# Moving the second memory's keys and values from the first projection stage into the differential attention

## The chip, the core and the metric

The kernel runs on one core of one Trainium2 chip, as one launch. The metric is the device time of the launch in microseconds (us). Three runs of the kernel before gave 3126.4, 3129.0 and 3129.66 us; their median, 3129.0 us, is the time before. Engines are named as the profile names them: PE is TensorE's matmul, PEld its weight load, DVE VectorE, ACT ScalarE, POOL GpSimd, SP SyncE, which issues most transfers here.

## What is computed

The reference is a chain of three blocks over 256 tokens of 1024 features. Only the first block is touched by the change. It has two layers: layer a with a differential attention, layer b with a gated recurrence. Both layers also attend to the same 256 memory rows, each with a norm gain and a projection of its own:

```python
def memory_attention(q_mem, mem, mem_norm_g, w_mem_kv):
    kv = rms_norm(mem, mem_norm_g) @ w_mem_kv          # 256 x 1024 @ 1024 x 512
    k, v = jnp.split(kv, 2, axis=-1)                   # 4 heads of 64
    s = jnp.einsum('bshd,bmhd->bhsm', q, k) * (MEM_HEAD_DIM ** -0.5)
    return einsum('bhsm,bmhd->bshd', softmax(s), v)

def diff_attention_mixer(h, mem, ...):                 # layer a
    q, k, v, qm = split(h @ w_in)                      # 768 + 768 + 768 + 256 columns
    o = rms_norm(diff_attention(q, k, v, lam, ...), subln_g) * (1 - lam_init)   # 6 heads, 2 softmaxes each
    om = memory_attention(qm, mem, a_mem_norm, a_w_mem_kv)
    return concat([o, om]) @ w_out

def hgrn2_mixer(h, mem, ...):                          # layer b, after a dense feed-forward
    ...
    om = memory_attention(qm, mem, b_mem_norm, b_w_mem_kv)
    return concat([o, om]) @ w_out
```

The keys and values of layer b's memory depend on nothing but the inputs, so they may be computed at any time before layer b's memory attention.

## The kernel before

The kernel is a row of stages. A stage is one block of instructions for every engine, written out by hand in the order in which each engine does them; between engines there are semaphores, and a stage begins on an engine only when all engines have ended the stage before it (in the trace this wait reads `PEq L171` or the like). Nothing is reordered by a scheduler.

Weights come through one stream (class `Stream`). Every 1024 x 512 piece of a weight matrix is a panel of 2 MB. SP loads panels in the order in which `s.add(...)` lists them into a ring of three slots (L305); the load of a panel waits until the panel three before it has been used. Since products are made of two rounded parts each, ACT copies half a panel, 128x2048, into `w_hi` (L349, `round_weights`), DVE subtracts that from the panel and writes the rest to `w_lo` (L358, `rest_of_weights`), and PE makes three passes: high by high, high by low, low by high (L470, `products`). Two buffers hold the two halves of a panel, so half 0 of the next panel can be prepared once half 0 of this one has been multiplied. The last thing a stage prepares is half 0 of the next stage's first panel (`first_of_next`); half 1 is prepared when the next stage opens (`open_stage`). A finished panel lies in a pair of PSUM banks and is copied out by ACT or DVE (`evict`).

The stages in question, in their order:

- `setup`: loads, constants, and the rounded parts of the memory under both gains, `mem_a_hi/lo` and `mem_b_hi/lo`. PE ends it with 54 transposes of the identity that compute nothing (`turn_identity`, L597).
- `mem_kv`: two panels, `a_w_mem_kv` and `b_w_mem_kv`, each 96 matmuls of 128x256: first 48 that give keys (kind F), then 48 that give values (kind T). Beside them stand the steps of `input_scales`: the sums of squares of the input x (ACT L828), after the first panel, and the roots (ACT L840), the reciprocal (DVE L846) and the scaled identity `diag` (DVE L849), after the second.
- `in_a`: turns x into features, 32 matmuls with `diag` (PE L689), rounds them (ACT L707, DVE L714), then multiplies five panels of `a_w_in`, 480 matmuls.
- `diff_attention` (function `attention`): 16 units, 12 of the differential attention (two softmaxes for each of six heads) and 4 of layer a's memory. The engines go through iterations s = 0, 1, 2, ... On PE iteration s holds the scores of unit s (L1273), the turned probabilities of unit s-2 (L1291) and the product with the values of unit s-3 (L1303). On DVE it holds mask and maximum of unit s (L1326, L1332; L1337 for memory units), then the reciprocal and scaling of unit s-1 (L1353, L1359). On ACT it holds the exponentials of unit s (L1396), the copy of the turned probabilities of unit s-2 (L1407) and the copy-out of a finished head (L1415). Scores lie in three PSUM banks in turn, 0, 1 and 6. At s = 2 PE makes 18 transposes of the identity.
- `out_a`: the heads are normalised and two panels of `a_w_out` are multiplied; then `dense`, layer b and the other two blocks follow.

Of the kernel before, what the change touches and what calls it, by code (L numbers as in the profile page):

```python
# [29 lines left out]
ALU = mybir.AluOpType  # L30
# [213 lines left out]
class Stream:  # L244
# [10 lines left out]
    def __init__(self, k):  # L255
        self.k = k
        self.jobs = []
        self.starts = []
        self.flat = []
        self.groups = self.halves = self.pairs = self.elsewhere = 0  # L260
        self.split_last = (0, 0)
        self.at = 0

    def add(self, runs):
        self.jobs.append(runs)
        self.starts.append(len(self.flat))
        for r in runs:

            r.first, r.group, r.halves, r.pairs = len(self.flat), self.groups, self.halves, self.pairs
            r.elsewhere = self.elsewhere  # L270
# [6 lines left out]
            self.groups += r.count // r.acc if r.kind not in ("experts", "routed") else 0  # L277
# [142 lines left out]
    def products(self, pe, m, by_chunk=False):  # L420
# [10 lines left out]
        for h in range(max(r.parts, 1)):  # L431
            kind = r.kinds[h]
# [8 lines left out]
            for o in range(width // P if kind == "F" else r.tiles):  # L441
                if r.kind == "R":
# [33 lines left out]
            if h == 0 and r.parts == 2:  # L476
                last.then_inc(k.first_half_used, 1)
        last.then_inc(k.panel_used, 1)

    def stage(self, name, side=None, extra=(), source=(), features=None, norm=False, heads=None,  # L480
# [7 lines left out]

        def evict(eng, m, which):
            r = m.r  # L490
            if r.on == which and m.j % r.acc == r.acc - 1:
                eng.wait_ge(k.panel_used, m.number + 1)
                q = m.p if r.acc == 1 else m.j // r.acc
                r.evict(nc, k.ps[:, 2 * m.bank:2 * m.bank + 2, :], q).then_inc(k.group_read[m.bank], 1)

        with stage(k, name) as st:
# [77 lines left out]
            @st.block.scalar  # L574
            def _(act):
                self.each_with_next(act, runs, lambda m, halves=(0, 1): self.round_weights(act, m, halves),
                                    lambda m: evict(act, m, "act"), steps.get("act", {}))

            @st.block.vector
            def _(dve):  # L580
                self.each_with_next(dve, runs, lambda m, halves=(0, 1): self.rest_of_weights(dve, m, halves),
                                    lambda m: evict(dve, m, "dve"), steps.get("dve", {}), evict_first=norm)
# [285 lines left out]
def input_scales(k, st):  # L868
# [3 lines left out]
    return {"act": {2: [lambda: squares(0, k.x, junk), lambda: squares(1, k.x, junk)], 3: [roots]},  # L872
            "dve": {2: [first_half], 3: [scales]}}
# [348 lines left out]

def unit(scores, values, scale=1.0, mask=None, causal=False, n=S, factor=None, floor=False):
# [15 lines left out]
def attention(k, name, groups, work, last_turns=0, scaled=True):  # L1239
# [14 lines left out]
    score_banks = (0, 1, 6)  # L1254

    with stage(k, name) as st:
        scores_ready, neg_max_ready, exp_done = st.sem("scores_ready"), st.sem("neg_max_ready"), st.sem("exp_done")
        norms_ready, transposed, pt_ready = st.sem("norms_ready"), st.sem("transposed"), st.sem("pt_ready")
        values_done, out_read, dve_order = st.sem("values_done"), st.sem("out_read"), st.sem("dve_order")

        def scores_of(s):
            return k.ps[:, score_banks[s % 3], :]

        @st.block.tensor
        def _(pe):
            for s in range(n_units + 3):
                if s < n_units:
                    u = units[s][0]
                    if s >= 3:
                        pe.wait_ge(exp_done, s - 2)  # L1270
# [24 lines left out]
                if s >= 3:  # L1295
# [4 lines left out]
                    if first and g >= 2:  # L1300
                        pe.wait_ge(out_read, g - 1)
                    for b, rows, first_token, to in u.blocks:
                        last = nc.tensor.matmul(k.ps[r0:r0 + dv, 4 + g % 2, first_token:S], u.values(b),  # L1303
# [4 lines left out]
            turn_identity(k, last_turns, 7)  # L1308

        @st.block.vector  # L1310
        def _(dve):
            o = Order(dve, dve_order)

# [55 lines left out]
            def outputs(m):  # L1369
                u, g, _, is_last = units[m]  # L1370
                if is_last and groups[g][4] is not None:
                    _, r0, dv, dst, gate = groups[g]
                    dve.wait_ge(values_done, m + 1)
                    nc.vector.tensor_tensor(dst, k.ps[r0:r0 + dv, 4 + g % 2, 0:S], gate,
                                            ALU.mult).then_inc(out_read, 1)

            for s in range(n_units + 4):
# [4 lines left out]
                if s >= 4:  # L1382
                    outputs(s - 4)

        @st.block.scalar
        def _(act):
            for s in range(n_units + 4):
# [21 lines left out]
                if s >= 4:  # L1409
                    m = s - 4  # L1410
                    u, g, _, is_last = units[m]
                    if is_last and groups[g][4] is None:
                        _, r0, dv, dst, _ = groups[g]
                        act.wait_ge(values_done, m + 1)
                        nc.scalar.activation(dst, k.ps[r0:r0 + dv, 4 + g % 2, 0:S], ACT.Copy).then_inc(out_read, 1)  # L1415
# [900 lines left out]
def plan_block1(k, w):  # L2316
# [24 lines left out]
    for i, m in enumerate("ab"):  # L2341
# [3 lines left out]
    s.add(runs)  # L2345
# [7 lines left out]
                                                       half_features(v.qm, scale=0.125)), halves="TF")])  # L2353
    s.add([run("T", w["a_w_out"], 0, v.cat_parts[1:], add_to_residual(k.x), on="dve", count=2, pieces=lambda p: 0)])
# [338 lines left out]
def block1(k, w, c, v):  # L2693
# [14 lines left out]
    attention(k, "diff_attention", groups + memory_groups(k, v.qm, v.km[0], v.vm[0], v.cat), v.work)  # L2708
# [1101 lines left out]
def build(nc, w, c, out, parts=(1, 2, 3)):  # L3810
# [45 lines left out]
    k.group_read = [nc.alloc_semaphore(f"group_read{i}") for i in range(SLOTS)]  # L3856
# [58 lines left out]
```

## Time and profile before

| | us |
|---|---|
| median of three runs | 3129.0 |
| lowest and highest run | 3126.4, 3129.66 |
| span of the profiled execution | 3122.5 |
| stage `mem_kv` on PE, its first matmul to its last | 31.41 to 55.90 |
| stage `in_a` on PE, first `diag` matmul to the last product | 58.74 to 120.87 |
| stage `diff_attention` on PE, from its first score matmul | from 122.69 |

The profile is of one execution. Its page gives the span from the first instruction to the last, 3122.5 us; the three timed runs lie 3.9 to 7.2 us above it, since what stands around the program is in a run's time and not in the span. Over the span PE is busy 97%, DVE 64%, ACT 48%. PE's busy time is modelled from pipelined matmuls, so where it matters the starts of instructions are read, not their ends. A row of the timeline gives the start, the length, the engine, the line, the operation, the tiles and, in brackets, how long the engine was idle before it and what released it.

### The profile page before, as it was taken

The numbers are of one execution on the slowest core, as the hardware profiler recorded it, in microseconds if no ns is written. First come the engines' busy times: TensorE is split into PE (matmuls) and PEld (weight loads), VectorE is DVE, ScalarE is ACT, GpSimd is POOL, SyncE is SP. The second block draws the span as 40 slices with busy tenths as digits, with TensorE's granted clock in tenths as the row PEclk, the third lists the DMA queues.
The fourth block names the chain that finished last, engine by engine and source line by source line (L and its number), as shares of the span: only waits on it lengthen the run. The fifth ranks groups of instructions, "written<-read, shape, count | busy, mean of one in ns | idle before, by whom it ended". The sixth has DMA issues, their size and how long they took to land. (4 is left out here: it accounts for less than half of the span.)

```text
span 3122.5 us, 43115 instructions
## 1 busy us (share of the span) xinstructions
PE 3014.5 (97%) x17959; PEld 2637.2 (84%) x17959; DVE 2007.9 (64%) x2237; ACT 1512.8 (48%) x1692; POOL 24.1 (1%) x41
## 2 busy tenths in 40 slices
PE   7999998899999999999999999999999999999998
PEld 6889897788888899778888888998789798997898
DVE  4547647555455467498898987554555756787755
ACT  4543343334344345477777776443434445432453
POOL 0001000000000000000000000000000000000000
PEclk9999999999999999999999999999999999999999
DMA  5338650065555567599999998541445143345142
GB/s 194 132 124 265 223 185 28 9 242 189 188 189 184 173 211 243 201 361 351 354 363 350 370 349 298 174 145 60 141 167 177 42 162 135 135 152 177 55 169 95
DMA packets 197852, 606.10 MB, mean 194 GB/s; under 512 B 19648, under 2 KB 59401, under 8 KB 154394
## 3 DMA queue, kind: packets, MB, share of 16 engines
q1 hardware_dynamic: 192306, 588.23, 53.0%
q0 software_dynamic: 3872, 12.71, 1.3%
q8 instruction: 142, 2.33, 0.3%
q10 hardware_dynamic: 1480, 2.41, 0.3%
q14 instruction: 52, 0.43, 0.0%
HBM read 602.26 MB, written 1.05 MB: 193 GB/s over the span
## 5 line engine op out<-in xcount | busy, mean ns | idle before, releaser
L2121 DVE TENSOR_TENSOR w_lo<-ring,w_hi 128x2048 fp32r<-128x2048 f32 x336 | 769.7, 2292 | 336.2 <-ACT w_hi L2016 331.0
L2016 ACT ACTIVATE w_hi<-ring 128x2048 fp32r<-128x2048 f32 x336 | 643.1, 1915 | 367.4 <-PE ps L1963 153.4
L358 DVE TENSOR_TENSOR w_lo<-ring,w_hi 128x2048 fp32r<-128x2048 f32 (+2 forms) x209 | 469.4, 2247 | 480.1 <-ACT w_hi L349 479.4
L349 ACT ACTIVATE w_hi<-ring 128x2048 fp32r<-128x2048 f32 (+2 forms) x209 | 392.7, 1881 | 645.1 <-PE ps L470 488.4
L470 PE MATMUL ps<-h_hi,w_hi 128*128 128x256 f32 x1616 | 463.7, 287 | 17.6 <-DVE w_lo L358 10.7
L470 PE MATMUL ps<-h_lo,w_hi 128*128 128x256 f32 x1616 | 459.7, 284 | 0.0
L470 PE MATMUL ps<-h_hi,w_lo 128*128 128x256 f32 x1616 | 459.5, 284 | 0.0
L470 PEld LDWEIGHTS ps<-h_hi,w_hi 128*128 128x128 f32 x1616 | 312.5, 193 | 22.2 <-issue 17.0
L470 PEld LDWEIGHTS ps<-h_lo,w_hi 128*128 128x128 f32 x1616 | 312.6, 193 | 0.3
L470 PEld LDWEIGHTS ps<-h_hi,w_lo 128*128 128x128 f32 x1616 | 312.6, 193 | 0.0
L1926 PE MATMUL ps<-w_hi,h_hi 128*128 128x512 f32 x672 | 266.6, 397 | 1.4 <-DVE w_lo L2121 1.4
L1926 PE MATMUL ps<-w_hi,h_lo 128*128 128x512 f32 x672 | 262.4, 390 | 0.0
L1926 PE MATMUL ps<-w_lo,h_hi 128*128 128x512 f32 x672 | 261.6, 389 | 0.0
L1926 PEld LDWEIGHTS ps<-w_hi,h_lo 128*128 128x128 f32 x672 | 126.1, 188 | 27.2
L1926 PEld LDWEIGHTS ps<-w_hi,h_hi 128*128 128x128 f32 x672 | 126.2, 188 | 26.2 <-DVE w_lo L2121 1.7
L1926 PEld LDWEIGHTS ps<-w_lo,h_hi 128*128 128x128 f32 x672 | 126.4, 188 | 24.9
L1926 PE MATMUL ps<-w_hi,picked_one_hi 128*128 128x512 f32 x336 | 135.4, 403 | 3.9 <-DVE w_lo L2121 3.9
L597 PE MATMUL ps<-ident 128*128 128x128 f32 x1076 | 128.7, 279 | 4.0 <-PEq L171 4.0
L1926 PE MATMUL ps<-w_hi,picked_one_lo 128*128 128x512 f32 x336 | 132.3, 394 | 0.0
L1926 PE MATMUL ps<-w_lo,picked_one_hi 128*128 128x512 f32 x336 | 131.5, 391 | 0.0
L597 PEld LDWEIGHTS ps<-ident 128*128 128x128 f32 x1076 | 122.8, 144 | 8.8 <-issue 7.4
L3280 DVE SCALAR_TENSOR_TENSOR arena<-arena,cols 128x256 f32<-128x256 f32 x288 | 119.8, 481 | 1.5
(539 smaller groups left out, 5544.3 us busy)
## 6 DMA issues: line engine op xcount, KB each, us to landing
ring<-in_moe_w_gate_up SPq DMA_DIRECT2D x224, 1024.0 KB, 4.9
ring<-in_moe_w_down SPq DMA_DIRECT2D x112, 1024.0 KB, 4.9
ring<-in_w_in SPq DMA_DIRECT2D x58, 1024.0 KB, 6.9
ring<-in_w_in_even SPq DMA_DIRECT2D x30, 1024.0 KB, 6.9
ring<-in_dense_w_gate_up SPq DMA_DIRECT2D x22, 1024.0 KB, 7.7
ring<-in_w_in_odd SPq DMA_DIRECT2D x16, 1024.0 KB, 6.7
arena<-in_w_ada POOLq DMA_DIRECT2D x24, 512.0 KB, 4.9
ring<-in_b_w_in SPq DMA_DIRECT2D x12, 1024.0 KB, 6.2
```

Of the source, the lines that this page charges most:

```text
L349: k.nc.scalar.activation(self.part(k.w_hi, b, m), src, ACT.Copy).then_inc(k.hi_ready, 1)
L358: k.nc.vector.tensor_tensor(self.part(k.w_lo, b, m), src, self.part(k.w_hi, b, m).bitcast(F32), ALU.subtract).then_inc(k.lo_ready, 1)
L470: last = nc.tensor.matmul(out, lhs, rhs, start=(opens and c == 0 and i == 0), stop=(closes and c == nk - 1 and i == len(passes) - 1 and (r ...
L597: k.nc.tensor.transpose(k.ps[:, bank, 0:P], k.ident[:, :], k.ident[:, :])
L1926: last = nc.tensor.matmul(k.ps[:, u % 3, :], xs[:, 4 * h + kk, at], w[:, kk, :], start=(h == 0 and kk == 0 and i == 0), stop=(h == 1 and k ...
L2016: nc.scalar.activation(high(g, h), raw(g, h), ACT.Copy).then_inc(k.hi_ready, 1)
L2121: nc.vector.tensor_tensor(low(g, h), raw(g, h), high(g, h).bitcast(F32), ALU.subtract).then_inc(k.lo_ready, 1)
L3280: ins = engine.scalar_tensor_tensor(out[:, c, :], src, w, out[:, c, :], ALU.mult, ALU.add)
```

## The change

The two memory projections are no longer one list of panels. The first, of layer a, is the only panel of `mem_kv`. The second, of layer b, becomes a list of its own between `in_a` and `out_a`, marked as an aside: no stage is built for it, it has a PSUM bank pair of its own (banks 6 and 7), and `attention` does its work in the iterations that `slots = [1, 1, 8, 8]` names: both blocks of keys (48 matmuls) on PE in iteration 1, both blocks of values (48 matmuls) in iteration 8.

With it, in `diff_attention`: ACT and DVE open with half 1 of the memory panel; after iteration 1 they prepare half 0 of `out_a`'s first panel; ACT copies the keys and values out at the end of iteration 9; scores use two PSUM banks instead of three, so the scores of unit s wait for the exponentials of unit s-2 instead of s-3; the 18 transposes of the identity at s = 2 are gone; SP issues in this stage the load that follows in the ring. In `mem_kv`, where only one panel is left, all steps of `input_scales` stand ahead of it.

```diff
@@ Stream.add
-    def add(self, runs):
+    def add(self, runs, aside=False):
@@ Stream.place
-        m.bank, m.before = group % SLOTS, i + group // SLOTS
+        m.bank, m.before = (SLOTS, r.asides + j) if r.aside else (group % SLOTS, i + group // SLOTS)
@@ input_scales
-    return {"act": {2: [lambda: squares(0, k.x, junk), lambda: squares(1, k.x, junk)], 3: [roots]},
-            "dve": {2: [first_half], 3: [scales]}}
+    return {"act": {1: [lambda: squares(0, k.x, junk), lambda: squares(1, k.x, junk), roots]},
+            "dve": {1: [first_half, scales]}}
@@ class Aside (new)
+    def products(self, pe, s):
+        for (q, h, o), at in zip(self.blocks, self.slots):
+            if at == s:
+                self.stream.products(pe, self.place(q), only=(h, o))
+    def prepare(self, s, split):
+        for j in range(2, 2 * len(self.panels) + 1):
+            if self.slots[2 * (j - 2) + 1] != s:
+                continue
+            if j < 2 * len(self.panels):
+                split(self.place(j // 2), (j % 2,))
+            else:
+                self.stream.first_of_next(split)
+    def evict(self, eng, s, which):
+        for q in range(len(self.panels)):
+            if self.slots[4 * q + 3] + 1 == s:
+                self.stream.evict(eng, self.place(q), which)
@@ attention
-    score_banks = (0, 1, 6)
+    score_banks = (0, 1) if aside else (0, 1, 6)
+    held = len(score_banks)
...
+        if aside:
+            @st.block.sync
+            def _(sp):
+                k.stream.ahead(sp)
...
-                    if s >= 3:
-                        pe.wait_ge(exp_done, s - 2)
+                    if s >= held:
+                        pe.wait_ge(exp_done, s - held + 1)
...
+                if aside:
+                    aside.products(pe, s)
...
-                    if m == 0:
+                    if m == 0 and not aside:
                         turn_identity(k, 18, 7)
...
+            if aside:
+                k.stream.open_stage(split)
             for s in range(n_units + 4):
...
+                if aside:
+                    aside.prepare(s, split)
+                    aside.evict(act, s, "act")
@@ plan_block1
-    s.add(runs)
+    s.add(runs[0:1])
     s.add([run("F", w["a_w_in"], 0, k.h, to_features(v.qk, scale=0.125)),
...
+    s.add(runs[1:2], aside=True)
@@ block1
-    attention(k, "diff_attention", groups + memory_groups(k, v.qm, v.km[0], v.vm[0], v.cat), v.work)
+    attention(k, "diff_attention", groups + memory_groups(k, v.qm, v.km[0], v.vm[0], v.cat), v.work,
+              aside=Aside(s, [1, 1, 8, 8]))
```

Line numbers move with the change: L349, L358, L828, L840, L1326 and L1396 of before are L351, L360, L836, L848, L1404 and L1488 of after.

ACT in stage `mem_kv`, before (L349 rounds weights, L828 are the sums of squares, L636 and L647 copy a panel out, L840 are the roots, L171 ends the stage):

```order
L574 UNCONDITIONAL_BRANCH
L349 ACTIVATE w_hi<-ring 128x2048 x2
L636 ACTIVATE arena<-ps 128x512
L647 ACTIVATE arena<-ps 128x512
L828 ACTIVATE ps,stat<-x_tokens 128x512 x4
L349 ACTIVATE w_hi<-ring 128x2048
L636 ACTIVATE arena<-ps 128x512
L647 ACTIVATE arena<-ps 128x512
L840 ACTIVATE stat<-stat 128x1 x2
L171 UNCONDITIONAL_BRANCH
```

The same place after:

```order
L582 UNCONDITIONAL_BRANCH
L836 ACTIVATE ps,stat<-x_tokens 128x512 x4
L848 ACTIVATE stat<-stat 128x1 x2
L351 ACTIVATE w_hi<-ring 128x2048
L644 ACTIVATE arena<-ps 128x512
L655 ACTIVATE arena<-ps 128x512
L171 UNCONDITIONAL_BRANCH
```

Two of the three roundings of weights and one copy-out have left the stage, and the roots have moved from its end to its start.

DVE at the start of `diff_attention`, before (L1326 adds the mask, L1332 takes the maximum, L1353 and L1359 scale the probabilities):

```order
L1310 UNCONDITIONAL_BRANCH
L1326 TENSOR_TENSOR ps<-ps,arena 128x384
L1332 TENSOR_REDUCE soft<-ps 128x1 x2
L1326 TENSOR_TENSOR ps<-ps,arena 128x384
L1332 TENSOR_REDUCE soft<-ps 128x1 x2
L1353 RECIPROCAL soft<-soft 128x2
L1359 TENSOR_SCALAR xn<-xn,soft 128x256
L1359 TENSOR_SCALAR xn<-xn,soft 128x128
L1326 TENSOR_TENSOR ps<-ps,arena 128x384
```

The same place after:

```order
L1385 UNCONDITIONAL_BRANCH
L360 TENSOR_TENSOR w_lo<-ring,w_hi 128x2048
L1404 TENSOR_TENSOR ps<-ps,arena 128x384
L1410 TENSOR_REDUCE soft<-ps 128x1 x2
L1404 TENSOR_TENSOR ps<-ps,arena 128x384
L1410 TENSOR_REDUCE soft<-ps 128x1 x2
L1431 RECIPROCAL soft<-soft 128x2
L1437 TENSOR_SCALAR xn<-xn,soft 128x256
L1437 TENSOR_SCALAR xn<-xn,soft 128x128
L360 TENSOR_TENSOR w_lo<-ring,w_hi 128x2048
L1404 TENSOR_TENSOR ps<-ps,arena 128x384
```

Two subtractions of half a panel now stand in DVE's queue, one ahead of unit 0 and one ahead of unit 2; on ACT a rounding of half a panel (L351) stands at the same two places.

## Rows read from the trace of the kernel before

**Rows 1.** Windows: stretch, length, busy and count of each engine, PEclk, DMA share, GB/s.

```profile
44.70:56.20 11.50, 11.47 (x96) 11.27 (x94) 4.67 (x3) 7.35 (x12) 0.00 (x0) 1.00 0.53 184
122.60:162.80 40.20, 37.02 (x199) 27.25 (x200) 27.69 (x94) 26.05 (x92) 0.00 (x0) 1.00 0.16 52
139.65:144.06 4.41, 4.24 (x23) 3.30 (x22) 3.70 (x13) 2.86 (x12) 0.00 (x0) 1.00 0.01 4
```

**Rows 2.** Timeline of PE: start, length, engine, line, operation; stage `mem_kv` into `in_a`.

```profile
31.41 0.49 PE L470 MATMUL ps<-mem_a_hi,w_hi 128*128 128x256 f32 x1 [4.19 <-PEq L171]
...
44.38 0.28 PE L470 MATMUL ps<-w_hi,mem_a_lo 128*128 128x256 f32 x1
...
55.90 0.28 PE L470 MATMUL ps<-w_hi,mem_b_lo 128*128 128x256 f32 x1
58.74 5.44 PE L689 MATMUL ps<-diag,x_tokens 128*128 128x128 f32 x32 [2.57 <-PEq L171]
63.94 0.36 PE L470 MATMUL ps<-h_hi,w_hi 128*128 128x256 f32 x1
```

**Rows 3.** Timeline of ACT in stage `mem_kv`: a rounding, and the end.

```profile
39.00 1.92 ACT L349 ACTIVATE w_hi<-ring 128x2048 fp32r<-128x2048 f32 x1 [10.70 <-PE ps L470]
...
56.70 0.59 ACT L647 ACTIVATE arena<-ps 128x512 f32<-128x512 f32 x1
57.18 0.48 ACT L840 ACTIVATE stat<-stat 128x1 f32<-128x1 f32 x2
```

**Rows 4.** Timeline of PE: the end of `in_a` and the start of `diff_attention`.

```profile
120.87 0.28 PE L470 MATMUL ps<-h_hi,w_lo 128*128 128x256 f32 x1
122.69 1.54 PE L1273 MATMUL ps<-arena 64*128 64x256 f32 x12 [1.54 <-PEq L171]
124.17 2.18 PE L597 MATMUL ps<-ident 128*128 128x128 f32 x18
...
128.67 0.55 PE L1291 MATMUL ps<-ident,xn 128*128 128x128 f32 x3 [0.59 <-DVE xn L1359]
```

**Rows 5.** Windows: granted clock after the gap at 58.74, and its longest low stretch.

```profile
59.00:62.00 3.00, 3.00 (x15) 3.00 (x15) 0.33 (x1) 0.84 (x2) 0.00 (x0) 0.50 1.05 408
...
482.00:493.00 11.00, 11.00 (x56) 11.00 (x57) 3.77 (x4) 6.60 (x5) 0.00 (x0) 0.53 0.00 0
```

**Rows 6.** Timeline of PE: the same turning into features ahead of the dense stage.

```profile
200.97 3.81 PE L689 MATMUL ps<-diag,x_tokens 128*128 128x128 f32 x32 [0.50 <-PEq L171]
204.54 0.36 PE L1559 MATMUL ps<-h_hi,w_hi 128*128 128x256 f32 x1
```

**Rows 7.** Timeline of ACT: the last rounding of `in_a`, and the start of `diff_attention`.

```profile
115.49 1.92 ACT L349 ACTIVATE w_hi<-ring 128x2048 fp32r<-128x2048 f32 x1 [2.99 <-PE ps L470]
...
122.65 1.28 ACT L1396 ACT_TABLE_LOAD   x1 [0.38 <-PEq L171]
124.88 0.47 ACT L1396 ACTIVATE xn<-ps,soft 128x256 f32<-128x256 f32 x1 [0.95 <-DVE soft L1332]
...
126.00 0.47 ACT L1396 ACTIVATE xn<-ps,soft 128x256 f32<-128x256 f32 x1 [0.21 <-DVE soft L1332]
```

**Rows 8.** Timeline of DVE: subtractions of half a panel, and the start of `diff_attention`.

```profile
117.44 2.29 DVE L358 TENSOR_TENSOR w_lo<-ring,w_hi 128x2048 fp32r<-128x2048 f32 x1 [3.52 <-ACT w_hi L349]
123.62 0.57 DVE L1326 TENSOR_TENSOR ps<-ps,arena 128x384 f32<-128x384 f32 x1 [3.88 <-PE ps L1273]
...
126.54 0.56 DVE L1326 TENSOR_TENSOR ps<-ps,arena 128x384 f32<-128x384 f32 x1
```

**Rows 9.** Timeline of PE, iterations 5 and 6 of `diff_attention`: the settled rhythm.

```profile
133.08 0.55 PE L1291 MATMUL ps<-ident,xn 128*128 128x128 f32 x3 [0.18 <-DVE xn L1359]
...
134.40 0.92 PE L1273 MATMUL ps<-arena 64*128 64x256 f32 x4
```

**Rows 10.** Timeline of ACT, iterations 4 and 5: the last part of unit 4's exponentials.

```profile
132.92 0.20 ACT L1396 ACTIVATION_READ_ACCUMULATOR xn<-ps,soft 128x1 f32 x1
...
134.19 0.48 ACT L1396 ACTIVATE xn<-ps,soft 128x256 f32<-128x256 f32 x1 [0.69 <-DVE soft L1332]
```

More of the change, by code:

```diff
@@ L259, in __init__ @@
         self.flat = []
-        self.groups = self.halves = self.pairs = self.elsewhere = 0
+        self.groups = self.halves = self.pairs = self.elsewhere = self.asides = 0
         self.split_last = (0, 0)
         self.at = 0
-    def add(self, runs):
+    def add(self, runs, aside=False):
         self.jobs.append(runs)
@@ L276, in add @@
             self.flat += [(r, p) for p in range(r.count)]
-            self.groups += r.count // r.acc if r.kind not in ("experts", "routed") else 0
+            self.asides += r.count if aside else 0
+            self.groups += r.count // r.acc if r.kind not in ("experts", "routed") and not aside else 0
             self.halves += r.count * r.parts
@@ L431, in products @@
         for h in range(max(r.parts, 1)):
+            if only and h != only[0]:
+                continue
             kind = r.kinds[h]
@@ L441, in products @@
             for o in range(width // P if kind == "F" else r.tiles):
+                if only and o != only[1]:
+                    continue
                 if r.kind == "R":
@@ L475, in products, with evict @@
                     last = nc.tensor.matmul(out, k.ones_row[0:1, 0:P], row, start=False, stop=True)
-            if h == 0 and r.parts == 2:
+            if h == 0 and r.parts == 2 and (not only or only == (0, 1)):
                 last.then_inc(k.first_half_used, 1)
-        last.then_inc(k.panel_used, 1)
+        if not only or only == (1, 1):
+            last.then_inc(k.panel_used, 1)
+    def evict(self, eng, m, which):
+        k, r = self.k, m.r
+        if r.on == which and m.j % r.acc == r.acc - 1:
+            eng.wait_ge(k.panel_used, m.number + 1)
+            q = m.p if r.acc == 1 else m.j // r.acc
+            r.evict(k.nc, k.ps[:, 2 * m.bank:2 * m.bank + 2, :], q).then_inc(k.group_read[m.bank], 1)
     def stage(self, name, side=None, extra=(), source=(), features=None, norm=False, heads=None,
@@ L1219, with __init__, place, all_read @@
 WHOLE = (0, S)
+class Aside:
+    def __init__(self, stream, slots, late=0, late_parts=None):
+        self.stream, self.slots, self.late, self.late_parts = stream, slots, late, late_parts
+        self.panels = [(r, p) for r in stream.jobs[stream.at] for p in range(r.count)]
+        self.blocks = [(q, h, o) for q in range(len(self.panels)) for h in range(2) for o in range(2)]
+        assert len(slots) == len(self.blocks) and all(r.parts == 2 for r, _ in self.panels)
+    def place(self, q):
+        r, p = self.panels[q]
+        return self.stream.place(r, 0, p)
+    def all_read(self, eng):
+        m = self.place(len(self.panels) - 1)
+        eng.wait_ge(self.stream.k.group_read[m.bank], m.before + 1)
+    def first_read(self, eng):
+        m = self.place(0)
+        eng.wait_ge(self.stream.k.group_read[m.bank], m.before + 1)
+    def products(self, pe, s):
[5 more added lines that the diff above has]
+            if self.slots[2 * (j - 2) + 1] != s:
+                continue
+            if j < 2 * len(self.panels):
[6 more added lines that the diff above has]
+                self.stream.evict(eng, self.place(q), which)
 def unit(scores, values, scale=1.0, mask=None, causal=False, n=S, factor=None, floor=False):
@@ L1236, in unit, with attention @@
     return u
-def attention(k, name, groups, work, last_turns=0, scaled=True):
+def attention(k, name, groups, work, last_turns=0, scaled=True, aside=None):
     nc = k.nc
@@ L1253, in attention, with out_of, gated @@
     diagonals = work[:, 4:6, :].rearrange("p b (t n) -> p b t n", t=TT)
-    score_banks = (0, 1, 6)
+    score_banks = (0, 1) if aside else (0, 1, 6)
+    held = len(score_banks)
+    late = aside.late if aside else 0
+    def out_of(g):
+        _, r0, dv, _, _ = groups[g]
+        return k.ps[r0:r0 + dv, 4 + g % 2, 0:S]
+    def gated(g):
+        return groups[g][4] is not None and g >= late
     with stage(k, name) as st:
@@ L1300, in _ @@
                     if first and g >= 2:
-                        pe.wait_ge(out_read, g - 1)
+                        if g - 2 < late:
+                            pe.wait_ge(out_copied, g - 1)
+                        else:
+                            pe.wait_ge(out_read, g - 1 - late)
                     for b, rows, first_token, to in u.blocks:
-                        last = nc.tensor.matmul(k.ps[r0:r0 + dv, 4 + g % 2, first_token:S], u.values(b),
+                        last = nc.tensor.matmul(out_of(g)[:, first_token:S], u.values(b),
                                                 exps_t[0:rows, m % 2, to:to + S - first_token],
@@ L1411, in _ @@
                     u, g, _, is_last = units[m]
-                    if is_last and groups[g][4] is None:
-                        _, r0, dv, dst, _ = groups[g]
+                    if is_last and not gated(g):
+                        dst = groups[g][3]
                         act.wait_ge(values_done, m + 1)
-                        nc.scalar.activation(dst, k.ps[r0:r0 + dv, 4 + g % 2, 0:S], ACT.Copy).then_inc(out_read, 1)
+                        nc.scalar.activation(dst, out_of(g), ACT.Copy).then_inc(out_copied if late else out_read, 1)
+                if aside:
+                    aside.prepare(s, split)
+                    aside.evict(act, s, "act")
+    if aside:
+        k.stream.at += 1
 def swiglu_run(w_gate_up, w_down, experts, ff):
```

40 lines of the change are left out of this document (23 added, 17 removed).

## The prediction, made before the changed kernel ran

> **What bounds the kernel now.** I read the busy times by stretch first, then PE's timeline through the three stages that the change touches, then ACT's and DVE's beside it. In `mem_kv` PE has matmuls without a break: in the 11.5 us of the second panel it is busy 11.47 us and ACT and DVE are not half busy [rows 1]. So a panel there costs what PE takes for it, and everything else hides under it. In `diff_attention` PE is busy 37.02 of 40.20 us, and in two settled iterations 4.24 of 4.41 us [rows 1]; its only wait there is 0.18 us for DVE's scaling [rows 9]. The waiting is at the start: 18 empty transposes of 2.18 us, and 0.59 us of idleness for DVE's scaling [rows 4]. So the attention is a chain from PE to DVE to ACT to PE at its start, and bound by PE after three iterations. The change takes 96 matmuls from a place where PE bounds and puts 48 where PE waits and 48 where PE bounds. Over the whole span there is nothing to be had beyond this: the rest of the order is unchanged.
>
> **What leaves `mem_kv`.** The second panel's matmuls begin with the one after 44.38 and the last begins at 55.90 [rows 2]: 96 matmuls, 11.52 us, all on the path. Its roundings lay under the first panel and cost nothing there.
>
> **The turn from `mem_kv` to `in_a`.** From the last matmul to the first of L689 it is 55.90 to 58.74, 2.84 us [rows 2]. In it ACT copies the panel out and then makes the roots, from 57.18 [rows 3], and DVE makes `diag`; only then do the engines meet. The roots and `diag` now stand ahead of the one panel, where ACT had no work until 39.00, for 10.70 us [rows 3], 7.6 of them after the stage's first matmul at 31.41 [rows 2], and DVE waits for ACT; so what is left is the copy-out. The turn from `in_a` to `diff_attention` has just that, a last panel copied out in two halves: 120.87 to 122.69, 1.82 us [rows 4]. Gain 1.02 us.
>
> **The clock behind this turn.** After the 2.57 us of idleness before 58.74 PE is granted 0.50, the 1.2 GHz level [rows 5], and L689 lasts 5.20 us until the first product at 63.94 [rows 2]. The same 32 matmuls ahead of the dense stage, after a gap of 0.50 us, take 3.57 us, 200.97 to 204.54 [rows 6]. The gap will be about 1.54 us, as at 122.69, and there the next stretch stayed at 1.00 [rows 1, 4]. I take the gain, 1.63 us; its other end is 0. Together the first product of `in_a` comes 11.52 + 1.02 + 1.63 = 14.17 us earlier. SP's loads move up with it; the first panel of `in_a` takes the ring slot of the memory panel, and its load is issued earlier than before.
>
> **The start of `diff_attention`.** All times here are on the clock of before. ACT's first instruction there begins at 122.65 [rows 7]. That is now half 1 of the memory panel; the subtraction on DVE starts 1.95 us after such a rounding (115.49 to 117.44) and holds DVE 2.29 us, some 2.2 us to the next start [rows 7, 8]. So the first mask starts at 122.65 + 1.95 + 2.2 = 126.8 instead of 123.62 [rows 8]: 3.2 us late. The first exponentials start 1.26 us after the first mask and the second 1.12 us after those [rows 7, 8], so 129.2, and last some 0.9 us: 130.1. Now ACT rounds half 0 of `out_a`'s first panel. It needs the buffer of the key half, so it waits for PE's first 48 matmuls; these start at about 123.7, behind two of the three score groups, and take 11.52 / 2 = 5.76 us: 129.5. They are in time, by 0.6 us, and cost nothing; without that cover each microsecond more would be one more here. ACT starts at 130.1, DVE subtracts at 132.05, and the mask of unit 2 follows at 134.25 instead of 126.54 [rows 8]: **7.7 us late**. Behind DVE's wait stand the scaling of unit 1 and with it PE's second group of transposes, which came 2.13 us after that mask, at 128.67 [rows 4]; now it comes at 136.4. PE has run out of work at about 131.6 (scores 2 and 3 and the first transposes, 2.1 us, after 129.5), so it is idle some 4.8 us.
>
> **The clock behind this stall.** Gaps of 4.19 us at 31.41 and 2.57 us at 58.74 [rows 2] were followed by the low level; this one is longer. At 58.74 the low stretch lost 1.63 us of work. In the attention the units that run in it are bound by PE, so I take 1.6 us, with 0 and 3.4 us (twice the stretch) as ends.
>
> **The second lump.** In iteration 8 PE makes 48 matmuls, 5.76 us, before the transposes of unit 6; ACT and DVE wait for the scores of unit 9. PE had 0.17 us of slack in 4.41 us [rows 1], so nearly all of it is on the path: **5.7 us**. The copy-out in iteration 9 is two ACT instructions of 0.5 us; ACT had 0.69 us of idleness in an iteration [rows 10], so 0.3 us, ends 0 and 1.0.
>
> **Scores in two banks.** Scores of unit 6 start at 134.40 [rows 9]; the exponentials of unit 4, which they will wait for, end at 132.92 + 0.20 = 133.12 [rows 10]. With 1.28 us to spare this costs nothing. SP's load in this stage waits for the second lump; its panel is used only in the dense stage, from 204.54 [rows 6], and lands long before.
>
> **The sum.** Earlier by 14.2, later by 7.7 + 1.6 + 5.7 + 0.3 = 15.3: 1.1 us more. It is made on an execution with a span of 3122.5 us, and the runs lie some 6.5 us above that span at their median; I add it to the median, 3129.0 + 1.1 = **3130.1 us**. What is late at the end of the attention stays late, since `out_a` begins when all engines have ended. A low stretch of the clock more or fewer in a later stage, whose phase moves, would be worth 1.6 us either way.
>
> A rule weighed. In these 40.20 us PEld is busy 27.25 us against PE's 37.02 [rows 1]. The Trainium skill, "Perfetto Trace Analysis", section "Identifying the Most-Contended Engine", says that the busy share of matmuls is no good measure of how close TensorE is to its limit, and that the share of weight loads is to be used. By it the attention would have room for the second lump, and the sum would be the first rival below; the 0.18 us of PE's waiting speaks against it, and the sum goes by that.
>
> **Rivals.**
> 1. *The second lump hides.* PE's weight loads leave 40.20 - 27.25 = 12.95 us in the attention [rows 1], more than a lump. Were that usable, the lump would cost nothing: 15.3 - 5.7 = 9.6 against 14.2, so 3129.0 - 4.6 = 3124.4 us, still within the bound. Against it: engines take their instructions in order, and PE's next start follows the last nearly at once [rows 9].
> 2. *The clock stays low.* PE restarts at 136.4 on a thin diet and keeps the 1.2 GHz level through iterations 4 to 8, as it did for 11 us at 482 to 493 [rows 5]. An iteration's PE work is 2.1 us (half of 4.24) and would be 4.2 against the 2.2 of now: 2.0 us for each of some four more iterations, 8 us: 3138.1 us, **slower**. It decides from the point where the low stretch is some 10 us longer than the one I count. For it: such a stretch exists. Against it: the settled attention ran at 1.00 with PE 96% busy [rows 1].
> 3. *The stall is not paid.* If later iterations took the 7.7 + 1.6 us back, the time would be 3120.8 us, **faster**. For it: ACT has 0.69 us idle in an iteration. Against it: PE would have to run ahead, and its slack over the twelve units is six times 0.17, 1 us.
>
> **How the numbers follow.** Forecast 0.81, rival 1 0.07, rival 2 0.08, rival 3 0.04. A measurement of this kernel tells changes from 0.2%, 6.3 us, on: 3122.7 to 3135.3. Forecast and rival 1 lie within; of the forecast's own spread I give nothing to either side. So faster 0.04, same 0.88, slower 0.08. Bounds: with the stall's clock loss at 0, copy-out 0, the lump at 4.9 (5.7 less 0.17 of slack in each of five pairs of iterations) and a low stretch fewer later, 14.2 - 12.6 + 1.6 = 3.2 us less, 3125.8. With the gain of the first clock term at 0, the second at 3.4, copy-out 1.0 and a low stretch more, 12.5 against 17.8 + 1.6: 6.9 more, 3135.9. Range 3125.8 to 3135.9.
>
> **What would show it.** In the changed profile: the last matmul of `mem_kv` at about 44.4 and L697 about 1.8 us later at full clock (the line of L689 will move by eight); a third mask of the attention about 7.7 us later, counted from the stage's start; a hole in PE of 4 to 5 us ahead of the second group of transposes, then a granted clock of 0.5; iteration 8 longer by 5.7 us. I am wrong if PE has no hole there, if iteration 8 is not longer, or if anything past `out_a` takes another time than before.

## The result, and the profile after

The changed kernel takes 3134.84 us at its median (3131.32 to 3139.34), the kernel before 3127.14 us (3122.53 to 3129.66) over six runs, the three of the forecast among them. The ratio is 1.0033, 95% interval 1.002 to 1.0046: slower, by 7.7 us. The forecast was 3130.1 us with a range of 3125.8 to 3135.9, and called the difference too small to measure. The time lies in the range; the call was wrong. Counted from the time of before, the range went from 3.2 us less to 6.9 us more, and 7.7 us lies outside it: the time falls inside because the kernel before came out 1.9 us lower over six runs than the 3129.0 us of the forecast, which is luck.

The table sets three points of PE's timeline side by side: the first product of `in_a`, the first score of `diff_attention`, and the first empty transpose of `out_a`, which begins when the attention has ended. Times are microseconds from the start of the profiled execution.

| | before | after | difference |
|---|---|---|---|
| first product of `in_a` | 63.94 | 48.32 | -15.6 |
| first score of `diff_attention` | 122.69 | 107.02 | -15.7 |
| end of `diff_attention` | 162.77 | 169.47 | +6.7 |
| length of `diff_attention` | 40.08 | 62.45 | +22.4 |
| span | 3122.5 | 3129.5 | +7.0 |

So nearly the whole difference is made before 170 us: 15.6 us won up to `in_a`, 22.4 us lost in the attention. The end of the attention in the kernel before, which [rows 4] don't show:

```profile
162.77 0.84 PE L597 MATMUL ps<-ident 128*128 128x128 f32 x6 [0.78 <-PEq L171]
```

PE's timeline of the kernel after, at these places (start, length, engine, line, operation; in brackets the idle time before it and what ended it; the answers to [rows 2] and [rows 4]):

```profile
44.76 3.81 PE L697 MATMUL ps<-diag,x_tokens 128*128 128x128 f32 x32 [1.50 <-PEq L171]
48.32 0.36 PE L476 MATMUL ps<-h_hi,w_hi 128*128 128x256 f32 x1
...
107.02 0.93 PE L1343 MATMUL ps<-arena 64*128 64x256 f32 x8 [1.48 <-PEq L171]
107.88 0.39 PE L476 MATMUL ps<-mem_b_hi,w_hi 128*128 128x256 f32 x1
...
114.67 0.55 PE L1363 MATMUL ps<-ident,xn 128*128 128x128 f32 x3
...
120.60 0.90 PE L1363 MATMUL ps<-ident,xn 128*128 128x128 f32 x3 [4.54 <-DVE xn L1437]
...
124.29 0.90 PE L1363 MATMUL ps<-ident,xn 128*128 128x128 f32 x3
...
139.04 0.58 PE L476 MATMUL ps<-w_hi,mem_b_hi 128*128 128x256 f32 x1
...
146.41 0.49 PE L1363 MATMUL ps<-ident,xn 128*128 128x128 f32 x3
...
169.47 0.85 PE L605 MATMUL ps<-ident 128*128 128x128 f32 x6 [0.78 <-PEq L171]
```

The turn from `mem_kv` to `in_a` has a gap of 1.50 us where it had 2.57, and its 32 matmuls last 3.56 us to the first product, at full clock. The first lump, the 48 matmuls of the keys, begins at 107.88, and the first transposes follow it at 114.67. Then PE waits 4.54 us for DVE's scaling. From there on one iteration takes 124.29 - 120.60 = 3.69 us, not the 2.2 us of before (4.41 us for two in [rows 1]), and the three transposes of an iteration 0.90 us, not 0.55. The second lump, the 48 matmuls of the values, takes 146.41 - 139.04 = 7.37 us.

Where the 4.54 us come from stands in DVE's timeline of the kernel after (the answer to [rows 8]; L360 is the subtraction of half a panel, L1404 the mask):

```profile
108.94 2.29 DVE L360 TENSOR_TENSOR w_lo<-ring,w_hi 128x2048 fp32r<-128x2048 f32 x1 [4.82 <-ACT w_hi L351]
111.15 0.56 DVE L1404 TENSOR_TENSOR ps<-ps,arena 128x384 f32<-128x384 f32 x1
...
116.27 2.29 DVE L360 TENSOR_TENSOR w_lo<-ring,w_hi 128x2048 fp32r<-128x2048 f32 x1 [2.12 <-ACT w_hi L351]
118.48 0.56 DVE L1404 TENSOR_TENSOR ps<-ps,arena 128x384 f32<-128x384 f32 x1
```

The third mask starts at 118.48, 11.46 us after the first score at 107.02. Before it was 126.54 - 122.69 = 3.85 us [rows 4, 8]. DVE waits 2.12 us for ACT's rounding and then subtracts for 2.29 us, and the scaling for which PE waits stands behind both.

The clock in the same stretch, by windows of the kernel after (stretch, length, busy time and count of PE, PEld, DVE, ACT and POOL, granted clock, DMA share, GB/s):

```profile
115.00:118.00 3.00, 1.06 (x7) 0.67 (x4) 1.73 (x1) 1.24 (x1) 0.00 (x0) 1.00 0.00 0
118.00:120.60 2.60, 0.00 (x0) 0.00 (x0) 2.50 (x9) 0.87 (x5) 0.00 (x0) 0.62 0.00 0
120.60:139.00 18.40, 18.40 (x55) 14.33 (x55) 9.23 (x32) 7.45 (x29) 0.00 (x0) 0.50 0.00 1
139.00:143.00 4.00, 4.00 (x21) 3.97 (x21) 1.97 (x7) 0.91 (x4) 0.00 (x0) 0.56 0.00 0
143.00:146.40 3.40, 3.40 (x30) 3.40 (x30) 0.00 (x0) 0.00 (x0) 0.00 (x0) 1.00 0.00 0
107.00:169.40 62.40, 56.14 (x276) 44.54 (x276) 32.51 (x96) 30.67 (x95) 0.00 (x0) 0.81 0.20 68
```

The clock falls inside the hole and stays at 0.50, the 1.2 GHz level, for all of the 18.4 us up to the second lump, though PE is shown busy for every one of them. It is back at 1.00 only between 3 and 4 us into that lump. DVE and ACT are each busy about half of that time or less: the stage waits for a slow PE.

The loss of 22.4 us then has three parts. The start is late by 11.46 - 3.85 = 7.6 us. Five iterations at 3.69 instead of 2.2 us cost 7.45 us. The second lump costs 7.37 us, of which 5.84 are its matmuls at full clock (measured below, with `out_a` prepared later) and 1.53 the low clock. The sum is 22.4.

### The profile page after: what moved, and what is told of

Read it like the earlier page. It is cut to its first block and busy times, and to the rows that moved or that the text cites. A ratio compares the mean times of both kernels' runs of the same rounds, so it can differ in the third digit from the quotient of the medians.

```text
span 3129.5 us, 43078 instructions
## 1 busy us (share of the span) xinstructions
PE 3020.2 (97%) x17941; PEld 2640.4 (84%) x17941; DVE 2008.0 (64%) x2237; ACT 1513.0 (48%) x1692; POOL 24.1 (1%) x41
## 5 line engine op out<-in xcount | busy, mean ns | idle before, releaser
L360 DVE TENSOR_TENSOR w_lo<-ring,w_hi 128x2048 fp32r<-128x2048 f32 (+2 forms) x209 | 469.4, 2247 | 475.0 <-ACT w_hi L351 474.3
L351 ACT ACTIVATE w_hi<-ring 128x2048 fp32r<-128x2048 f32 (+2 forms) x209 | 392.7, 1881 | 633.7 <-PE ps L476 474.9
L476 PEld LDWEIGHTS ps<-h_hi,w_hi 128*128 128x128 f32 x1616 | 312.6, 193 | 20.9 <-issue 15.6
```

The lines of the kernel that those rows point to most:

```text
L351: k.nc.scalar.activation(self.part(k.w_hi, b, m), src, ACT.Copy).then_inc(k.hi_ready, 1)
L360: k.nc.vector.tensor_tensor(self.part(k.w_lo, b, m), src, self.part(k.w_hi, b, m).bitcast(F32), ALU.subtract).then_inc(k.lo_ready, 1)
L476: last = nc.tensor.matmul(out, lhs, rhs, start=(opens and c == 0 and i == 0), stop=(closes and c == nk - 1 and i == len(passes) - 1 and (r ...
```

## Experiments

The theory to be tested (A): the hole ahead of the second transposes takes the clock, and the attention's own matmuls, which keep a high clock, don't bring it back; without the hole, or with the clock brought back, only the late start and the second lump are lost. The rivals: the iterations are slow for another reason that the change brought (two score banks instead of three, preparations in the queues of ACT and DVE), or the attention would have fallen low by itself. All runs in one table; the first three number columns are from the profiled execution, in us.

| kernel | end of attention | its length | span | ratio to before, 95% |
|---|---|---|---|---|
| before | 162.77 | 40.08 | 3122.5 | |
| after | 169.47 | 62.45 | 3129.5 | 1.0033 (1.002 to 1.0046) |
| after, run again | 171.59 | 63.13 | 3130.0 | 1.0029 (1.0017 to 1.004) |
| after, hole filled | 163.09 | 53.48 | 3123.3 | 0.9997 (0.9989 to 1.0006) |
| after, `out_a` prepared later | 158.14 | 49.77 | 3119.4 | 0.9993 (0.9985 to 1.0002) |
| after, second lump earlier | 164.33 | 56.08 | 3125.1 | 1.0013 (1.0004 to 1.0022) |
| after, transposes behind the hole | 169.26 | 61.05 | 3127.6 | 1.0011 (1.0001 to 1.0021) |
| before, roots first | 160.71 | 40.58 | 3122.4 | 0.9992 (0.9983 to 1.0001) |
| before, with a hole | 187.98 | 65.23 | 3150.2 | 1.0081 (1.0066 to 1.0096) |

**The hole filled.** In the changed kernel PE gets 38 empty transposes of the identity, into a bank that nothing else uses then, ahead of its wait for the second scaling:

```diff
                     if m == 0 and not aside:
                         turn_identity(k, 18, 7)
+                    if m == 1 and aside:
+                        turn_identity(k, 38, 7)
```

> The changed kernel with 38 transposes of the identity on PE ahead of its second group of transposes, that is in the hole of 4.54 us in which PE waits for DVE; nothing else moves. 38 x 0.12 us = 4.6 us, so they end about when the hole ends. Theory A (the hole drops PE's clock, and the attention's thin work then leaves it at 1.2 GHz until the second lump): the granted clock stays at 1.00 through iterations 2 to 8, an iteration there takes 2.2 us instead of 3.69, and the kernel is some 6 us faster than the changed one: about 3128.5 against 3134.8. Theory B (the lumps and the two score banks keep PE's clock low, hole or not): clock 0.5 again, time within 1 us of the changed kernel's. Theory C (transposes of the identity fill PE's time and yet don't hold its clock): clock 0.5 from about the same place, as in B, and real products in the hole are the next thing to try.

PE's timeline, and the windows of the same stretch (columns as above):

```profile
118.59 4.37 PE L605 MATMUL ps<-ident 128*128 128x128 f32 x38
123.19 0.55 PE L1365 MATMUL ps<-ident,xn 128*128 128x128 f32 x3 [0.24 <-DVE xn L1439]
...
118.60:123.20 4.60, 4.36 (x40) 4.13 (x39) 4.23 (x9) 1.11 (x6) 0.00 (x0) 1.00 0.01 4
123.20:140.00 16.80, 16.44 (x103) 14.04 (x104) 11.02 (x39) 8.36 (x33) 0.00 (x0) 1.00 0.00 0
```

The transposes do nothing but keep PE at work. The second scaling comes no earlier for them, and yet the clock stays at 1.00 and the attention lasts 53.48 us, 9.0 less than in the profile of the changed kernel. What is left over the 40.08 us of before is 13.4: the 7.6 of the start and 5.8 for the lump. The ratio to before is 0.9997, so all of the measured loss is gone, with both lumps, both score banks and all preparations in place. That excludes the first rival. The gain of the change is gone too: it stands level with the kernel before.

**The preparation of `out_a` moved.** ACT rounds and DVE subtracts the first half of `out_a`'s first panel after iteration 7, under the second lump, instead of after iteration 1:

```diff
-            if self.slots[2 * (j - 2) + 1] != s:
+            if self.slots[2 * (j - 2) + 1] + 6 != s:
                 continue
```

> The changed kernel with one number altered: ACT and DVE prepare half 0 of out_a's first panel after iteration 7 instead of after iteration 1, so that it lies under the second lump. Theory A (the stall of DVE behind PE's first lump makes the hole, and the hole makes the long low stretch): no hole over 1 us, clock 1.00, the mask of unit 2 comes about 3.9 us later than before (behind the first lump) instead of 7.7, the attention costs 3.9 + 5.7 + 0.3 = 9.9 us more than before instead of 22, against 14 to 15.6 us gained ahead of it: 4 to 5.5 us faster than the kernel before, about 3122.5. Theory B (lumps keep the clock low): the stall goes but the clock is still 0.5, some 4 us faster than the changed kernel, about 3130.5.

PE's timeline, and windows from the attention's start to the second lump, and over the lump:

```profile
118.26 0.55 PE L1363 MATMUL ps<-ident,xn 128*128 128x128 f32 x3 [0.85 <-DVE xn L1437]
...
129.24 0.39 PE L476 MATMUL ps<-w_hi,mem_b_hi 128*128 128x256 f32 x1
...
135.08 0.49 PE L1363 MATMUL ps<-ident,xn 128*128 128x128 f32 x3
...
108.40:129.20 20.80, 19.59 (x122) 16.39 (x122) 16.17 (x49) 12.73 (x41) 0.00 (x0) 1.00 0.26 99
129.20:135.10 5.90, 5.90 (x50) 5.86 (x50) 3.46 (x5) 2.41 (x4) 0.00 (x0) 1.00 0.00 0
```

The hole shrinks to 0.85 us and the clock does not fall in the attention. The attention lasts 49.77 us, 9.7 more than before: 5.84 for the lump (129.24 to 135.08), and 3.9 by which the third mask is late (116.13 - 108.37 = 7.76 us after the first score, against 3.85 before). That mask no longer waits for a preparation but for PE's scores of its unit, which stand behind the first lump, as was expected:

```profile
116.13 0.57 DVE L1404 TENSOR_TENSOR ps<-ps,arena 128x384 f32<-128x384 f32 x1 [0.62 <-PE ps L1343]
```

The five iterations ahead of the lump take 129.24 - 118.26 = 10.98 us, 2.2 each, as before. In the profile the attention ends 4.6 us earlier than before and the span is 3.1 us shorter; the median is 3121.29 against 3124.58 us, but the interval of the ratio ends at 1.0002, so a gain on the kernel before is not told from none. On the changed kernel it is one: 0.9993 against 1.0033, with intervals that lie apart.

**The second lump moved up.** The two value blocks are projected in iteration 4 instead of 8:

```diff
-              aside=Aside(s, [1, 1, 8, 8]))
+              aside=Aside(s, [1, 1, 4, 4]))
```

> The changed kernel with the second lump, the 48 matmuls of the values, in iteration 4 instead of 8. The hole stays. Theory A, with the low stretch lasting until dense products come: the clock is back at 1.00 some 4 us into that lump, four iterations earlier, each of which then takes 2.2 instead of 3.69 us: 6 us faster than the changed kernel, about 3129, low stretch some 9 to 10 us long instead of 24. Rival (the stretch has its own length, whatever PE does in it): low for 24 us again, so time as the changed kernel's or up to 2 us longer, since the lump then runs at the low clock throughout.

```profile
121.83 0.90 PE L1363 MATMUL ps<-ident,xn 128*128 128x128 f32 x3 [4.54 <-DVE xn L1437]
...
121.80:125.50 3.70, 3.67 (x11) 2.88 (x11) 1.69 (x6) 1.75 (x7) 0.00 (x0) 0.50 0.02 4
125.50:128.00 2.50, 2.50 (x12) 2.48 (x12) 1.97 (x7) 0.92 (x4) 0.00 (x0) 0.51 0.00 0
128.00:132.40 4.40, 4.40 (x39) 4.40 (x38) 0.00 (x0) 0.00 (x0) 0.00 (x0) 1.00 0.00 0
132.40:150.00 17.60, 16.91 (x90) 13.13 (x88) 12.97 (x45) 10.98 (x41) 0.00 (x0) 1.00 0.37 120
```

The hole is the same 4.54 us, and the clock is lost the same way. It is back at 1.00 2.5 us into the lump, which now begins at 125.5 instead of 139.0, and stays there for the iterations behind it. The attention is 6.4 us shorter than in the changed kernel (56.08 against 62.45). So what ends the low stretch is the lump, wherever it stands, and not the number of iterations.

**The roots first, alone.** The kernel before with the one part of the change that moves the squares, roots and `diag` of `mem_kv` to its start; both panels stay there:

```diff
-    return {"act": {2: [lambda: squares(0, k.x, junk), lambda: squares(1, k.x, junk)], 3: [roots]},
-            "dve": {2: [first_half], 3: [scales]}}
+    return {"act": {1: [lambda: squares(0, k.x, junk), lambda: squares(1, k.x, junk), roots]},
+            "dve": {1: [first_half, scales]}}
```

> The kernel before with one part of the change: the sums of squares, roots and scales of the input stand ahead of the first panel of mem_kv; both memory panels stay there, and the attention is untouched. By the prediction's terms the turn into in_a takes 1.82 instead of 2.84 us, and the clock behind it stays at 1.00, which gives 1.0 + 1.6 us: 2.6 us faster than the kernel before, about 3124.5. Rival: ACT, which now rounds half 1 of the second panel after the sums, is late with nothing and nothing is gained but the 1.0 us, since the clock falls after any such turn: 3126.

```profile
57.81 3.81 PE L689 MATMUL ps<-diag,x_tokens 128*128 128x128 f32 x32 [1.50 <-PEq L171]
61.38 0.36 PE L470 MATMUL ps<-h_hi,w_hi 128*128 128x256 f32 x1
...
57.80:61.40 3.60, 3.59 (x33) 3.60 (x33) 1.53 (x4) 2.31 (x6) 0.00 (x0) 1.00 0.98 358
...
120.13 1.54 PE L1273 MATMUL ps<-arena 64*128 64x256 f32 x12 [1.54 <-PEq L171]
121.61 3.85 PE L597 MATMUL ps<-ident 128*128 128x128 f32 x18
125.29 0.49 PE L1291 MATMUL ps<-ident,xn 128*128 128x128 f32 x3
...
121.70:125.10 3.40, 3.40 (x17) 3.40 (x18) 3.29 (x11) 1.82 (x8) 0.00 (x0) 0.50 1.07 358
```

Against [rows 2] the gap is 1.50 instead of 2.57 us, and the first product of `in_a` comes at 61.38 instead of 63.94, 2.56 us earlier: the two terms of 1.02 and 1.63 us together. At the end of the attention 2.06 of them are left, and in the span 0.1. The last rows show why 0.5 us are lost in the attention: here the clock falls at its start, behind a gap of 1.54 us, and is back when the 18 empty transposes end, which take 3.85 us instead of the 2.18 of [rows 4]. So the attention can fall low without the hole, but with these transposes behind the fall it was low for 3.4 us only; they are among what the change takes out. The ratio, 0.9992 (0.9983 to 1.0001), agrees with 2.6 us but does not tell it from none.

**The changed kernel again**, in the runs of the next two:

> The changed kernel itself, once more, beside the two that follow and beside the kernel before. If the long low stretch of PE's clock is what the hole brings on every time, the new profile shows it again, from the hole to the second lump (some 24 us at 0.5), and the time is 6 to 8 us above the kernel before. Rival: the stretch was a chance of that one execution, and this one shows a short stretch of 3 to 7 us, with a time some 3 to 4 us lower.

It measured 1.0029 (1.0017 to 1.004) and repeats the picture: a gap of 4.54 us, the low level behind it, and the high one again only within the second lump. The first product of `in_a`, and windows behind the hole and at the lump's end:

```profile
49.77 0.36 PE L476 MATMUL ps<-h_hi,w_hi 128*128 128x256 f32 x1
...
122.00:145.00 23.00, 22.95 (x76) 18.83 (x77) 11.22 (x39) 8.41 (x33) 0.00 (x0) 0.50 0.00 1
146.00:149.00 3.00, 3.00 (x27) 3.00 (x26) 0.00 (x0) 0.00 (x0) 0.00 (x0) 1.00 0.00 0
```

**A hole in the kernel before.** Two subtractions whose result nothing reads go on DVE behind iteration 1; there is no lump, there are three score banks, and nothing is prepared:

```diff
                 if s >= 4:
                     outputs(s - 4)
+                if s == 1 and name == "diff_attention":
+                    for _ in range(2):
+                        o(nc.vector.tensor_tensor(k.w_lo[:, 1, :], k.w_hi[:, 1, :].bitcast(F32), ...
```

> The kernel before, with nothing of the change, and two idle subtractions of half a panel on DVE after iteration 1 of the differential attention (4.5 us, into a buffer that nothing reads before it is filled anew): a hole in PE of some 5 us at the place of the changed kernel's, with three score banks, 18 empty transposes and no lump anywhere. Theory (a hole drops the clock, and the attention's own work does not bring it back): low from about 128 to the end of the attention or to the next dense stretch, 12 iterations of 3.7 instead of 2.2 us: 4.5 + 15 to 18, some 20 us slower than the kernel before, about 3145. Rival (a low stretch of some 3.4 us, as I had predicted): 4.5 + 1.6, about 3131.

PE's timeline, and the windows of the hole, of the rest of the attention, and of its end:

```profile
133.38 0.90 PE L1291 MATMUL ps<-ident,xn 128*128 128x128 f32 x3 [5.24 <-DVE xn L1359]
...
127.20:133.40 6.20, 0.96 (x6) 0.69 (x5) 6.03 (x10) 0.90 (x5) 0.00 (x0) 0.87 0.25 79
133.40:183.00 49.60, 49.60 (x144) 36.52 (x145) 23.14 (x78) 19.52 (x73) 0.00 (x0) 0.50 0.00 1
183.00:188.00 5.00, 4.05 (x20) 2.00 (x18) 0.00 (x0) 2.64 (x7) 0.00 (x0) 1.00 0.00 0
```

A wait that made PE's transposes 4.7 us later (133.38 against 128.67 in [rows 4]) costs the attention 25.2 us, and the kernel 1.0081 (1.0066 to 1.0096). PE is shown busy for 49.60 of 49.60 us and is granted 0.50 in all of them. Here no lump comes, and the low level lasts until 183.0, 5 us before the stage's end; why it ends there isn't shown. The estimate, some 20 us, was 5 too small: it counted 12 iterations of 3.7 us, and the trace has 13 groups of transposes from the hole to 183.0, and four of the iterations are longer than 4 us. This excludes the second rival, since the same attention without the hole runs at 1.00 [rows 1], or with the roots first is low for 3.4 us at its start, and it shows that no other part of the change is needed for the loss.

**Transposes behind the hole.** The same 38 transposes as in the first experiment, one iteration later, when the clock has already fallen (the condition is `m == 2`):

> The changed kernel with 38 transposes of the identity on PE not in the hole but after it, ahead of the third group of transposes; the hole stays. If PE without a break brings the clock back, whatever it works on: some 4 us into the transposes the clock is at 1.00 again, the transposes cost 5.5 to 6 us, and iterations 4 to 8 take 2.2 us, which saves 6 to 7: within 1 us of the changed kernel. If only dense products do that, the clock stays at 0.5 until the second lump, the transposes take 8 to 9 us, and the kernel is some 8 us slower than the changed one, about 3142.

```profile
121.79 0.90 PE L1365 MATMUL ps<-ident,xn 128*128 128x128 f32 x3 [4.54 <-DVE xn L1439]
125.48 6.71 PE L605 MATMUL ps<-ident 128*128 128x128 f32 x38
132.02 0.49 PE L1365 MATMUL ps<-ident,xn 128*128 128x128 f32 x3
...
121.80:130.00 8.20, 8.20 (x32) 7.39 (x33) 3.62 (x13) 2.62 (x11) 0.00 (x0) 0.50 0.01 2
131.00:140.00 9.00, 8.88 (x53) 7.32 (x52) 5.25 (x18) 3.64 (x13) 0.00 (x0) 1.00 0.00 0
```

Transposes without a break between them bring the clock back as the lump does, and the attention's iterations keep it from then on. The transposes themselves take 6.71 us of PE, so the attention gains only 2.1 us on the changed kernel run beside it (61.05 against 63.13); within 1 us was expected. The median, 3129.42 against 3134.28 us, differs by more than the two profiles do (3127.6 against 3130.0), and the two ratios' intervals overlap a little; only the clock is shown here, not the size of the gain.

## Why the prediction was wrong, by its own steps

**What leaves `mem_kv`, the turn, and the clock behind it: right.** 11.52 + 1.02 + 1.63 = 14.17 us were forecast for the first product of `in_a`. The changed kernel run again has it at 49.77, 14.17 us earlier; the profile above has it at 48.32, 15.6 earlier, because there the first panel of `mem_kv` escaped a low stretch that it had before. The gap forecast at 1.54 us is 1.50, and the clock behind it holds. The start of `mem_kv` after, and the windows of it after and before (columns as above):

```profile
31.52 0.36 PE L476 MATMUL ps<-mem_a_hi,w_hi 128*128 128x256 f32 x1 [3.28 <-PEq L171]
...
31.00:35.00 4.00, 3.48 (x29) 3.51 (x30) 0.51 (x4) 3.16 (x10) 0.00 (x0) 1.00 0.94 352
...
31.00:35.00 4.00, 3.59 (x17) 3.62 (x18) 0.02 (x1) 0.00 (x0) 0.00 (x0) 0.57 0.89 317
```

**The start of `diff_attention`: right.** Forecast late by 7.7 us with an idle PE for some 4.8; measured 7.6 and 4.54.

**The clock behind this stall: this step failed.** It was sized at 1.6 us, at most 3.4, by the low stretch at 58.74, which is followed by 32 feature matmuls and the dense products of `in_a`, one after another. Measured are 7.45 us in five iterations and 1.53 in the lump, 9.0 us, which is also what the attention gains when the hole is filled. The row taken as the measure was of the wrong kind: what the low level costs depends on the work that follows it, and here that is work that does not bring the clock back. That possibility stood beside the forecast as rival 2, with 8 us for iterations 4 to 8, and got a chance of 0.08, on the ground that the settled attention ran at 1.00 with PE 96% busy [rows 1]. This row shows that the attention keeps a clock that it has. It says nothing of whether it regains one that it has lost, and the kernel with a hole alone shows that it doesn't, for 49.6 us. With 9.0 in the place of 1.6 the forecast's sum would have been 1.1 + 7.4 = 8.5 us. The spans differ by 7.0; most of the rest are the 1.4 us that the first panel won beyond the forecast. The low stretch at 482 to 493 [rows 5], which spoke for the rival, was the better row: there PE is shown busy for 11.00 of 11.00 us and is still low.

**The second lump: right.** Forecast 5.7 us on the path; 5.84 at full clock with `out_a` prepared later, which refutes rival 1. The Trainium skill, "Perfetto Trace Analysis", section "Identifying the Most-Contended Engine", would judge TensorE's headroom by the share of its peak that the matmuls reach, which the prediction leaves out, and by its weight loads. By the weight loads the lump had room; the runs don't agree, since 48 matmuls cost their full time in a stage whose weight loads left a third of it free.

**Copy-out and score banks: right.** After the second lump nothing beyond it is lost (9.7 us in the experiment with the later preparation, all of it named above), and with two banks five iterations take 2.2 us each.

**Rival 3, the stall not paid: refuted** by the hole filled, where the 7.6 us of the start are still in the attention's length though all runs at full clock.

**A low stretch more or fewer later: more than was allowed.** From the end of the attention to the end of the program the nine profiles differ from the one of before by up to 2.5 us (with the hole in the kernel before, 25.2 us at the end of the attention and 27.7 at the end); 1.6 us were allowed. Which of them come in an execution was not settled. The medians of the kernel before moved from 3124.58 to 3127.14 us between the runs, so of gains below some 3 us none was shown.

**What stays open.** Why PE's work in the attention holds the higher level but is so slow to regain it. The runs show that within 48 matmuls, or 38 or 18 transposes, in a row the clock comes back, and that 49.6 us of the attention's scores, transposes and values went by before it did. The trace shows no break in PE's work in either, and which of their differences decides was not tried.

## What to carry to other kernels

Work that is moved into a stage where engines take turns has to be priced by what its preparation does in the queues of the other engines: half a panel's rounding and subtraction held up the scaling, and PE with it, for some 4 us. Price such a hole in PE by the work behind it and not by its own length: look for a row in which such work brought the clock back, as 48 matmuls in a row did here, and if there is none, count the whole stretch up to the next work that does. The remedies are cheap: put the preparation where PE has work of its own (under the lump), or fill the hole with empty transposes, and read the granted clock by stretch before believing that a busy PE is a fast one. Either remedy took back the loss here; neither made the change a gain on the kernel before that could be told from none.

## What the runs showed of the hardware

The record of PE as busy for 49.60 of 49.60 us, at a granted clock of 0.50, was not expected; in the same stage and the same kernel, without the hole, it is busy 37.02 of 40.20 us at 1.00 [rows 1]. The hole of 4.54 us, in four profiles, and that of 5.24 us (the hole alone) were each followed by 0.50. That agrees with the advice of the Trainium skill, "TensorE: Matmul & The Clock Gate", section "Why this matters for your kernels", to avoid idle gaps between bursts of matmuls. The length of a gap alone does not tell what follows: behind the 2.57 us ahead of `in_a` in the kernel before the clock was at 0.50, behind the 3.28 us ahead of `mem_kv` in the changed kernel it stayed at 1.00, and behind the 1.54 us ahead of the attention it stayed at 1.00 in the kernel before and fell to 0.50 with the roots first. What else decides was not tried.

Empty transposes did for the clock what matmuls do: 38 of them in 4.37 us held it, and within 38 in 6.71 us, or 18 in 3.85 us, it came back.
